# Scores of the sample tokens in four column groups of the array, two batches to each

## What is computed

```
def memory_attention(q, mem_k, mem_v):
    b, l, _ = q.shape
    q = q.reshape(b, l, XA_HEADS, XA_HEAD_DIM)
    s = jnp.einsum('blhd,bmhd->bhlm', q, mem_k.astype(q.dtype)).astype(jnp.float32) * (XA_HEAD_DIM ** -0.5)
    p = jax.nn.softmax(s, axis=-1).astype(q.dtype)
    o = jnp.einsum('bhlm,bmhd->blhd', p, mem_v.astype(q.dtype))
    return o.reshape(b, l, XA_DIM)
```

## Time and profile before

| what | value |
| --- | --- |
| runs shown: median, lowest, highest | 3865.18, 3860.28, 3868.9 us |
| profiled execution, its own time | 3864.85 us |
| its span | 3863.1 us |
| mean granted clock of TensorE | 0.838 |
| PE busy | 3257.6 us, 84% |
| DVE busy | 1787.1 us, 46% |
| ACT busy | 622.4 us, 16% |
| HBM traffic over the span | 282 GB/s |

### The profile page before, as it was taken

The page is one execution under the profiler, slowest core; times in us unless marked ns, Lnnn a source line. Parts: engine busy times, 40 slices in busy tenths (PEclk is TensorE's granted clock), DMA queues, the critical chain, the costliest instruction groups (busy, mean ns, idle before and its releaser), DMA issues.

```text
span 3863.1 us, 51091 instructions
## 1 busy us (share of the span) xinstructions
PE 3257.6 (84%) x18104; PEld 2218.8 (57%) x18104; DVE 1787.1 (46%) x4190; ACT 622.4 (16%) x1638; POOL 818.5 (21%) x921
## 2 busy tenths in 40 slices
PE   8989999999998899999899999978765666665564
PEld 7767777777776679999787888745410000000000
DVE  2396655555564300002633333357964444444444
ACT  1001222222221100001111111122221111111111
POOL 1000221212211000000122222223233333333332
PEclk9999999999999889999999999979855555555555
DMA  5433323333331348887699999999999999999997
GB/s 193 145 132 116 113 90 107 113 105 108 107 102 61 126 143 290 294 288 259 259 419 419 417 419 417 419 407 417 393 360 419 418 416 418 416 415 414 415 416 301
DMA packets 201144, 1089.73 MB, mean 282 GB/s; under 512 B 27089, under 2 KB 68945, under 8 KB 73617
## 3 DMA queue, kind: packets, MB, share of 16 engines
q0 software_dynamic: 92160, 671.13, 42.3%
q1 hardware_dynamic: 101760, 394.97, 28.7%
q10 hardware_dynamic: 7120, 22.22, 1.5%
HBM read 1056.59 MB, written 31.65 MB: 282 GB/s over the span
## 4 chain that ended last, share of the span: by engine, by line
PE 53%; DMA 30%; DVE 10%; issue 5%; ACT 1%; POOL 0%; DVEq 0%; SPq 0%; ACTq 0%; POOLq 0%
DMA branches<-in_peer_u,idx 25%; PE psum L497 24%; PE psum L561 15%; DMA ring<-in_peer_u,idx 4%; DVE branches L1801 2%; DVE branches L1354 2%; PE psum L919 1%; DVE ring L1801 1%; PE psum L634 1%; PE psum L643 1%; PE psum L640 1%; PE psum L737 1%; PE psum L338 1%; PE psum L620 1%; PE psum L710 1%
## 5 line engine op out<-in xcount | busy, mean ns | idle before, releaser
L1801 DVE CUSTOM_DVE_ANT_0 ring<-ring,psum 128x1024 f32<-128x1024 f32 x480 | 566.9, 1219 | 653.9 <-DMA ring<-in_peer_u,idx 621.0
L497 PE MATMUL psum<-hT,ring 128*128 128x128 f32 (+2 forms) x4800 | 803.4, 328 | 30.2 <-DMA ring<-in_w_glu 11.7
L497 PEld LDWEIGHTS psum<-hT,ring 128*128 128x128 f32 x4800 | 719.9, 196 | 106.6 <-issue 32.7
L902 PE MATMUL psum<-shared,selb 24*128 24x512 bf16 x1280 | 306.9, 524 | 457.1 <-DVE dots L1801 453.9
L902 PEld LDWEIGHTS psum<-shared,selb 24*128 24x128 bf16 x1280 | 57.1, 96 | 1028.0 <-DVE dots L1801 939.8
L561 PE MATMUL psum<-hT,ring 128*128 128x320 f32 x2112 | 625.1, 435 | 9.6 <-DMA ring<-in_w_att 7.9
L561 PEld LDWEIGHTS psum<-hT,ring 128*128 128x128 f32 x2112 | 381.6, 191 | 142.2 <-issue 14.5
L1214 ACT ACTIVATE ge<-dots 128x1 f32<-128x1 f32 x320 | 94.4, 295 | 1507.8 <-DVE dots L1801 1507.8
L1801 DVE CUSTOM_DVE_ANT_0 branches<-branches,psum 128x1024 f32<-128x1024 f32 x160 | 189.0, 1219 | 250.9 <-DMA branches<-in_peer_u,idx 250.5
L497 PE MATMUL psum<-branches,ring 128*128 128x128 f32 (+1 forms) x2048 | 295.6, 303 | 6.2 <-ACT shared L1150 6.2
L497 PEld LDWEIGHTS psum<-branches,ring 128*128 128x128 f32 x2048 | 286.1, 192 | 9.9 <-issue 9.9
(11 more groups left out here) (387 smaller groups left out, 3323.4 us busy)
## 6 DMA issues: line engine op xcount, KB each, us to landing
ring<-in_w_merge SPq DMA_DIRECT2D x160, 1024.0 KB, 5.1
ring<-in_w_head SPq DMA_DIRECT2D x64, 1024.0 KB, 4.8
ring<-in_w_outp SPq DMA_DIRECT2D x32, 1024.0 KB, 7.0
ring<-in_w_pq SPq DMA_DIRECT2D x32, 1024.0 KB, 8.9
ring<-in_w_att SPq DMA_DIRECT2D x24, 1024.0 KB, 4.9
ring<-in_w_mem SPq DMA_DIRECT2D x16, 1024.0 KB, 4.7
ring<-in_w_glu SPq DMA_DIRECT2D x16, 1024.0 KB, 7.9
out_qkv_out<-ring ACTq DMA_DIRECT2D x16, 520.5 KB
```

The costliest lines, as they stand in the source:

```text
L497: last = mat(out, ring[:, j, (k0 + kt) * P:(k0 + kt + 1) * P], src[:, kt, :], start=kt == 0, stop=kt == kts - 1)
L902: last = mat(ps[q][:, :], selb[32 * q:32 * q + 24, j, :], hb[32 * q:32 * q + 24, g_, :], start=True, stop=True)
L1801: v.tensor_tensor_reduce(out=u, in0=u, in1=x, scale=1.0, scalar=0.0, op0=ALU.mult, op1=ALU.add, accum_out=dots[:, g_, j, half_:half_ + 1]) ...
```

## The change

The 64 sample tokens' scores are laid out in 128 rows ("slots") instead of 64. Row group q (rows 32q to 32q+31) holds batches 2q and 2q+1 in its first 16 rows, and 16 rows that no token uses. `qm` becomes, for each d and each c of 0 and 1, one block of 128 columns with the queries of batch 2q+c in columns 32q+8c to 32q+8c+7 and zeros elsewhere. A statement now has 32 columns of it as its stationary operand and writes 32 rows of bank 3; the order is d, c, then q, so that four statements in a row go to four row groups of the result. The number of statements (16) and of moving columns (256) stays. Both key tiles are reported done in the last four statements. The softmax of the samples runs over 128 rows, and several small instructions become one.

```diff
-                for b in range(NBATCH):
-                    for d in two:
-                        at_ = (b % 4) * 512 + d * MEM
-                        last = mat(ps[3][0:NS, 0:MEM], qm[:, d, b * NS:(b + 1) * NS], ring[:, 2 + b // 4, at_:at_ + MEM],
-                                   start=b + d == 0, stop=b == NBATCH - 1 and d == 1)
-                    if b % 4 == 3:
-                        last.then_inc(tiles_done, 1)
+                for d in two:
+                    for c in two:
+                        for q in range(4):
+                            b = 2 * q + c
+                            at_ = (b % 4) * 512 + d * MEM
+                            last = mat(ps[3][32 * q:32 * q + 32, 0:MEM], qm[:, d, c, 32 * q:32 * q + 32],
+                                       ring[:, 2 + b // 4, at_:at_ + MEM], start=d + c == 0, stop=d + c == 2, skip_group_check=True)
+                            if d + c == 2 and q % 2:
+                                last.then_inc(tiles_done, 1)
...
-                    last = nc.tensor.transpose(ps[7][:, m * NS:(m + 1) * NS], pp[0:NS, 2, m * P:(m + 1) * P], ident[0:NS, 0:NS])
+                    last = nc.tensor.transpose(ps[7][:, m * P:(m + 1) * P], pp[:, 2, m * P:(m + 1) * P], ident[:])
...
-            st(v.memset(seven[:, 0:2 * 576], 0.0))
+            st(v.memset(seven[:, 0:4 * P], 0.0))
...
                 for d in two:
-                    last = v.tensor_copy(qm[:, d, :].rearrange("p (b s) -> p b s", s=72)[:, :, 0:TS],
-                                         xqs[a % 2][:, d, TP:].rearrange("p (b s) -> p b s", b=NBATCH))
+                    for c in two:
+                        last = v.tensor_copy(qm[:, d, c, :].rearrange("p (q n) -> p q n", q=4)[:, :, c * TS:(c + 1) * TS],
+                                             xqs[a % 2][:, d, TP:].rearrange("p (q n) -> p q n", q=4)[:, :, c * TS:(c + 1) * TS])
...
-                st(v.tensor_reduce(mx[0:NS, 2:3], ps[3][0:NS, 0:MEM], AX, ALU.max))
+                st(v.tensor_reduce(mx[:, 2:3], ps[3][:, 0:MEM], AX, ALU.max))
                 st.wait()
-                v.tensor_scalar(mx[:, 0:2], mx[:, 0:2], -1.0 / 16.0, None, ALU.mult)
-                v.tensor_scalar(mx[0:NS, 2:3], mx[0:NS, 2:3], -1.0 / 16.0, None, ALU.mult).then_inc(mx_ready, 1)
+                v.tensor_scalar(mx[:], mx[:], -1.0 / 16.0, None, ALU.mult).then_inc(mx_ready, 1)
                 dve.wait_ge(pexp_ready, a + 1)
-                st(v.reciprocal(sm[:, 0:2], sm[:, 0:2]))
-                st(v.reciprocal(sm[0:NS, 2:3], sm[0:NS, 2:3]))
+                st(v.reciprocal(sm[:], sm[:]))
                 st.wait()
-                for t in range(UNITS):
-                    n = P if t < 2 else NS
-                    last = v.tensor_scalar(pp[0:n, t, :], pp[0:n, t, :], sm[0:n, t:t + 1], None, ALU.mult)
-                last.then_inc(pn_ready, 1)
+                v.tensor_tensor(pp, pp, sm[:].unsqueeze(2).to_broadcast([P, UNITS, MEM]), ALU.mult).then_inc(pn_ready, 1)
                 dve.wait_ge(pt_done, a + 1)
-                v.tensor_copy(pT[:, :, TP:], ps[7][:, 0:P].rearrange("p (m t) -> p m t", m=2)).then_inc(pt_ready, 1)
+                for m in two:
+                    last = v.tensor_copy(pT[:, m, TP:].rearrange("p (q n) -> p q n", q=4),
+                                         ps[7][:, m * P:(m + 1) * P].rearrange("p (q n) -> p q n", q=4)[:, :, 0:2 * TS])
+                last.then_inc(pt_ready, 1)
```

More of the change, by code:

```diff
@@ L240, in build @@
         xq, pp, pT = view(six, at, 2, TOKENS), view(six, at, UNITS, MEM), view(six, at, 2, TOKENS)
-        qm = seven[:, 0:2 * 576].rearrange("p (t n) -> p t n", t=2)
-        xqs = (xq, seven[:, 2 * 576:2 * 576 + 2 * TOKENS].rearrange("p (t n) -> p t n", t=2))
+        qm = seven[:, 0:4 * P].rearrange("p (t c n) -> p t c n", t=2, c=2)
+        xqs = (xq, seven[:, 4 * P:4 * P + 2 * TOKENS].rearrange("p (t n) -> p t n", t=2))
         mx, sm, r3 = sb("mx", [P, UNITS]), sb("sm", [P, UNITS]), sb("r3", [P, UNITS])
@@ L1080, in _ @@
                 for t in range(UNITS):
-                    n = P if t < 2 else NS
-                    src = ps[2][:, t * MEM:(t + 1) * MEM] if t < 2 else ps[3][0:n, 0:MEM]
-                    last = fn(pp[0:n, t, :], src, ACT.Exp, bias=mx[0:n, t:t + 1], scale=1.0 / 16.0, accum_out=sm[0:n, t:t + 1])
+                    src = ps[2][:, t * MEM:(t + 1) * MEM] if t < 2 else ps[3][:, 0:MEM]
+                    last = fn(pp[:, t, :], src, ACT.Exp, bias=mx[:, t:t + 1], scale=1.0 / 16.0, accum_out=sm[:, t:t + 1])
                 last.then_inc(pexp_ready, 1)
```

## The result

The changed kernel took 3839.59 us (median of four runs, 3836.91 to 3842.05) against 3863.33 us before; the ratio is 0.9931, with a 95% interval of 0.9919 to 0.9944. Timed twice more it was 0.9937 (0.9921 to 0.9953) and 0.9934 (0.992 to 0.9948). The 15 runs have a mean of 3841.2 us and 32 runs of the kernel before one of 3865.5: 24 us less, 2.6 us either way. One more execution of the kernel before, in a state of the chip in which the granted clock was 0.682, took 4490.59 us and is left out. The forecast was 3845, 20 us less.

The account below looks back on a forecast made before the run. PE was taken to bound the attention; 3864.85 - 20.5 (score blocks) + 0.1 (transposes) + 0 = 3844.5 us, 3844.8 after a 0.3 us adjustment to the runs' median, given as 3845, range 3837 to 3852.

Parts of the forecast that it names:

- the transposes' term of the sum: Attention: the widened sample-token transposes cost 0.05 us more for each of the last head's two, together +0.1 us.
- The clock's term of zero: Attention: shifted work moves where the clock falls in the output block; nothing in the sum, 3 us either way.
- The bound, and what passes to the end: PE decides in the attention, so a microsecond saved there is a microsecond at the end unless something becomes late.
- Four groups together: Score block: four column groups run at once, 1.9 us a head, 8.2 us in place of 28.80; gain taken as 20.5.
- A: Score block: half the overlap, 3.6 us a head, gain 13.8 us, 3851 us in all; chance 0.07.
- B: Score block: no overlap, the four groups run in turn as now, 3865 us; chance 0.03.
- C: Score block: the array drains at every change of column group, +10.2 us, 3875 us; chance 0.03.
- The softmax: Attention softmax on DVE and ACT: merged instructions change zero in sum, at most 0.1 us either way in the last head.
- the cover of head 0: Head 0's softmax ends before PE finishes the queries: margin shrinks from 6.3 to 1.2 us, nothing lost yet.
- rival D: Attention: head 0's wait, a ring tile or low-clock queries come late, 5 to 8 us in all, 3851; chance 0.07.
- the query tiles: Next queries' weights: first tile needed some 10 us after issue, against 4.9 us to landing (at most 10.0); no wait taken.

Follow-up runs that it names:

- the order experiments: Changed kernel with its 16 score statements reordered, one column group after another or groups in two alternating pairs: 3849.13 and 3850.48 us.
- the two orders and widths: Kernel before with the sample tokens' transposes as wide as the others, or narrow but placed after the four wide ones: 3867.48 and 3866.9 us.
- `late_softmax`: Changed kernel with two more VectorE passes over 1536 elements ahead of head 0's softmax: 3842.74 us.
- `gap_filled`: Changed kernel with seven statements of an unread product on PE in the gap of the last head's softmax: 3837.35 us.
- the next version, `values_ahead`: Changed kernel with the sample tokens' output also in four column groups and tiles issued up to six ahead: 3804.48 us.
- `values_too`: Changed kernel with the sample tokens' output also in four column groups, tiles still issued four ahead: 3807.34 us.

## Why the prediction was right in its main term, and which step failed

Forecast were 20 us, and the runs give 24, 2.6 us either way. **The step that failed is the transposes' term of the sum:** it was put at +0.1 us, as the price of more columns, and measured -1.6 us. With it the sum would have been close to the 22 us that the stage shows. The clock's term of zero came out by luck, as two shares that cancel. Some 2 us more are not placed, and their cause stays open.

**The bound, and what passes to the end: right.** PE's chain in the attention set the time, and the stages behind it moved with it. From the last L739 to the end of the span it was 2421.9, 2423.1 and 2422.8 us in the three profiles with the old score block, and 2419.4, 2423.2 and 2420.3 with the change: 1.6 us less, within the scatter of either.

**Four groups together: right.** Forecast were 1.9 us a head and 8.2 us in all; measured 1.86 with a high clock and 8.36 in all, a gain of 20.4 (forecast 20.5). The estimate from the figure for three groups in the Trainium skill's "TensorE: Matmul & The Clock Gate" (measured speedup) had 9.1 us. That heads which begin while the clock is low would keep a surplus was right in kind: 2.59 in head 1 for 1.86. Its size, 0.6 us in all, was 0.9 in this profile, and 2.0 and 1.6 in the two others of the change. Rivals A, B and C are excluded by 1.86 us and the order experiments; A had a true core, since PE's reach is limited, but eight records to each group did not bring it back in this order.

**The transposes: wrong in sign.** The step took L719's and L720's shares of the chain in the last head as the cost of their width, and "about 0.2 us" for both kinds in the others. In head 0 of the kernel before, the second pair of L719 took 0.37 us in the chain and the first 0.22. The pair behind a narrow transpose is the slow one, and the two orders and widths show that the change of shape is what costs; the step did not look for it. With all six alike the change took 0.34 us less in each of three heads and 0.6 in the last, where 0.25 of it is the clock's.

**The softmax: right**, 4.02 us for 4.00, and the cover of head 0 1.14 us for 1.2; `late_softmax` shows that the wait stands open behind it.

**The clock: a zero made of two terms.** It was put at zero, 3 us either way, for independent shifts. In the means of three profiles each, L739 of heads 0 to 2 gained 2.8 us (30.9 to 28.2), and the last one lost 3.1 (10.4 to 13.47), the same 13.47 in each of the three. They cancel, so the zero is right by luck: the loss is no scatter about zero. The idle time ahead of it has a part in it, as `gap_filled` shows; why it appeared only with the new block is open.

**The total.** The terms give 20.4 + 1.6 = 22 us, and the stage 22.4 in the profiled execution, 20.8 in the means of three profiles (155.6 to 134.8; two of the three with the old block have the cheaper transposes). The runs give 24, 2.6 us either way, so the forecast of 20 lies just outside, for the transposes it lacks and 2 us more. Those 2 us are not placed: no stage outside the attention shows them beyond its scatter.

**Nothing came late** (rival D): PE waited for no tile in the stage, until the next version made it over 30 us shorter; there, with the old issue order (`values_too`), the query tiles, named as the tightest, were the ones that did.

## What to carry to other kernels

Where a product is 64 columns wide or less and is repeated for several operands, its results can lie in four row groups of a bank, and four statements run in nearly the time of one (32 records in 1.86 us for 7.05); take turns between the groups statement by statement, since a group's statements in a row gave 4.52 us where turns gave 1.86. The zero padding of the stationary operand (two batches to a group) added no statement and no moving column here. And after such a gain look at the piece with few moving columns beside it: it held the clock low for its neighbours, and giving it the same layout took another 36 us off the stage, more than the first change.

## What the runs showed of the hardware

- Matmuls of different column groups start out of program order, within a reach of a few records: about 20 rounds for 32 records with one group after the other, 12 with two pairs, 8 with all four in turn.
- A change of shape between neighbouring f32 transposes, 64 rows with 64 moving columns beside 128 rows with 128, costs 0.1 to 0.15 us: six transposes took 0.67 us when all are wide, 0.72 when the two narrow ones come last, and 1.01 when they are mixed.
- Behind 64 records of 128 by 128 weights and 8 moving columns the granted clock went from 1.00 to 0.50 though PE was busy throughout (mean 0.60 over 11.2 us, of which 11.2 busy); with 32 records of 256 columns in four groups in their place it stayed at 1.00 over 83 us of `values_ahead`.
- With PE idle for 4.0 us the granted clock was 0.50 behind the gap, and the next 8 records took 3.78 us and the 64 behind them 13.47; with the gap filled it stayed at 1.00 at first, and they took 1.99 and 10.07. The 64 also took 10.4 us behind an unfilled gap in the kernel before, where the clock came back sooner.
